# From the router to the experts: a normalised row in halves, a weight piece split earlier, gate products begun on half of their input, and fills left out

## What is computed

```python
h2l = modulate(rms_norm(xl, norm_ffn[l]), sh2, sc2)
xl = xl + g2 * moe_ffn(h2l, w_router, b_router, *experts)
...
def moe_ffn(h, w_router, b_router, w_gate, w_up, w_down):
    aff = jax.nn.sigmoid((tok @ w_router).astype(jnp.float32))
    biased = (aff + b_router.astype(jnp.float32)).reshape(n_tok, N_GROUPS, EXPERTS_PER_GROUP)
    ...
    def expert_block(args):
        xb, e = args
        hb = jax.nn.silu(xb @ w_gate[e]) * (xb @ w_up[e])
        return hb @ w_down[e]
```

## Time and profile before

| | |
|---|---|
| runs | 2020.72, 2022.87, 2019.8 us |
| the profiled execution | 2017.9 us |
| its span | 2016.2 us |
| TensorE (PE) busy | 1964.6 us |
| VectorE (DVE) busy | 1717.3 us |
| ScalarE (ACT) busy | 1162.6 us |
| mean over the span, DMA | 312 GB/s |
| mean granted clock of TensorE | 0.995 |

### The profile page before, as it was taken

How to read it: one execution, slowest core, us unless ns; L and a number is a source line. 1 busy time by engine, 2 the same in 40 slices (tenths; PEclk the granted TensorE clock), 3 DMA queues, 4 the chain that set the end, 5 groups by cost and what they waited for, 6 DMA issues and landing times.

```text
span 2016.2 us, 25838 instructions
## 1 busy us (share of the span) xinstructions
PE 1964.6 (97%) x9392; PEld 1566.4 (78%) x9392; DVE 1717.3 (85%) x1731; ACT 1162.6 (58%) x1134; POOL 196.5 (10%) x254
## 2 busy tenths in 40 slices
PE   7999999999999999999999998999999999999996
PEld 3788558778888888888888577677888888888885
DVE  4775789898689999999999988777799999999997
ACT  2324613323367777777777355344477777777774
POOL 3000110111030000000000300100100000000001
PEclk9999999999999999999999999999999999999998
DMA  9766417666489999999999677286799999999995
GB/s 347 269 238 224 143 67 240 244 221 252 183 284 410 391 406 392 397 392 398 396 400 390 250 254 250 64 328 222 271 391 390 399 395 397 391 403 387 405 388 219
DMA packets 181489, 629.45 MB, mean 312 GB/s; under 512 B 13903, under 2 KB 16091, under 8 KB 174368
## 3 DMA queue, kind: packets, MB, share of 16 engines
q1 hardware_dynamic: 150648, 503.62, 66.1%
q0 software_dynamic: 27808, 119.98, 16.2%
q10 hardware_dynamic: 2952, 4.77, 0.6%
HBM read 597.13 MB, written 31.19 MB: 312 GB/s over the span
## 4 chain that ended last, share of the span: by engine, by line
PE 83%; DVE 9%; DMA 5%; ACT 2%; issue 1%; SPq 1%; POOL 0%; ACTq 0%; DVEq 0%; POOLq 0%
PE bank L2517 78%; PE bank L2527 4%; DVE work L1693 3%; DMA ring<-in_w_mod_dram 1%; DVE m_lo L1693 1%; DVE ring L1693 1%; PE bank L2790 1%; DMA ring<-in_w_in_dram 1%; DMA work<-hp_dram 1%; DMA ring<-in_w_exp_down_dram 1%; DVE work L2073 1%; DVE w_lo L1693 1%; DMA x<-in_ctx_dram 1%; DMA ring<-in_w_out_dram 1%; ACT work L1444 0%
## 5 line engine op out<-in xcount | busy, mean ns | idle before, releaser
L1693 DVE TENSOR_TENSOR w_lo<-ring,w_hi 128x2048 fp32r<-128x2048 f32 x384 | 873.6, 2289 | 87.8 <-ACT w_hi L1556 86.2
L1556 ACT ACTIVATE w_hi<-ring 128x2048 fp32r<-128x2048 f32 x384 | 738.0, 1922 | 237.1 <-PE bank L2517 232.1
L2517 PE MATMUL bank<-w_hi,xsT_hi 128*128 128x512 f32 x1024 | 399.8, 390 | 0.8 <-DVE w_lo L1693 0.6
L2517 PE MATMUL bank<-w_lo,xsT_hi 128*128 128x512 f32 x1024 | 398.6, 389 | 0.0
L2517 PE MATMUL bank<-w_hi,xsT_lo 128*128 128x512 f32 x1024 | 315.4, 389 | 0.0
L1276 ACT ACTIVATE m_hi<-ring 128x1024 fp32r<-128x1024 f32 (+1 forms) x128 | 129.8, 1031 | 262.2 <-PE bank L2517 211.9
L2517 PEld LDWEIGHTS bank<-w_hi,xsT_hi 128*128 128x128 f32 x1024 | 192.2, 188 | 44.9 <-issue 1.9
L2517 PEld LDWEIGHTS bank<-w_hi,xsT_lo 128*128 128x128 f32 x1024 | 192.2, 188 | 40.2
L2517 PEld LDWEIGHTS bank<-w_lo,xsT_hi 128*128 128x128 f32 x1024 | 192.2, 188 | 38.6
L2517 PE MATMUL bank<-w_hi,hexpT_hi 128*128 128x512 f32 x512 | 202.3, 395 | 0.6 <-DVE w_lo L1693 0.6
L2517 PE MATMUL bank<-w_lo,hexpT_hi 128*128 128x512 f32 x512 | 199.5, 390 | 0.0
(11 more groups left out here) (304 smaller groups left out, 2634.5 us busy)
## 6 DMA issues: line engine op xcount, KB each, us to landing
ring<-in_w_exp_gate_dram SPq DMA_DIRECT2D x128, 1024.0 KB, 9.1
ring<-in_w_exp_up_dram SPq DMA_DIRECT2D x128, 1024.0 KB, 7.9
ring<-in_w_exp_down_dram SPq DMA_DIRECT2D x128, 1024.0 KB, 8.6
ring<-in_w_in_dram SPq DMA_DIRECT2D x44, 1024.0 KB, 7.3
work<-in_w_mod_dram POOLq DMA_DIRECT2D x40, 1024.0 KB, 5.6
ys_dram<-work POOLq DMA_DIRECT2D x32, 512.0 KB, 7.8
work<-hp_dram SPq DMA_DIRECT2D x54, 256.0 KB, 4.4
work<-mod_dram POOLq DMA_DIRECT2D x8, 1024.0 KB, 9.5
```

Of the source, the lines that this page charges most:

```text
L1556: nc.scalar.activation(w_hi[:, pos % N_SPLIT, :], raw(i), ACT.Copy).then_inc(hi_done, 1)
L1693: return nc.vector.tensor_tensor(o, a, b, op)
L2517: return nc.tensor.matmul(o, a, b, start=first, stop=last)
```

## The change

Eight edits.

1. `in_halves` is true for layer 0's last block alone. There `modulated_halves` makes the row in two halves of 512 columns, counting a new semaphore `half_row` for the first and `rows_ready` for the second; `turn_row` waits for each in turn.
2. For the same block `high(0, 0)` stands in front of the squares in ScalarE's order, and waits for `split_used` (two quarters of the last output products are done) in place of `dve_took`.
3. `logits` waits for each half of `hT` before its four matmuls, for all blocks and layers.
4. The two fills in front of layer 0's last logits are dropped.
5. `gate_up` of expert 0 waits for the first half of `xt_lo` before piece 0 and for the second before piece 2, in both layers; its three fills are dropped.
6. In layer 1 the two fills between the merged rows' transposes are dropped.
7. In layer 1 the two fills in front of each half of block 0's output products are dropped.
8. The semaphore `zero_rows` goes; its one use counts on `zero_ready`.

```diff
+def in_halves(l, k):
+
+    return l == 0 and k == len(tokens_of(l)) - 1
...
-                    nc.gpsimd.memset(ys[:, 1, :], 0.0).then_inc(zero_rows, 1)
-                    pool.wait_ge(zero_rows, 1)
+                    nc.gpsimd.memset(ys[:, 1, :], 0.0).then_inc(zero_ready, 1)
+                    pool.wait_ge(zero_ready, 3)
...
+                    if isinstance(e, int) and e == 0 and p == 0 and turned_gates(l):
+                        act.wait_ge(split_used, 3 * SPLIT_NO[("o", l, 1)] + 2)
+                    elif isinstance(e, int) and ready_at(e, p) <= N_SPLIT:
...
                 for k, tb in enumerate(T):
+                    if in_halves(l, k):
+                        high(0, 0)
                     act.wait_ge(dve_took, TAKEN[("o", l, 1, tb)])
                     square_of(2 * l + 1, k, tb, h2row[k])
...
-                high(0, 0)
+                if not in_halves(l, len(T) - 1):
+                    high(0, 0)
...
+            def modulated_halves(row, k, tb):
+
+                ends = (half_row, rows_ready)
+                for n in range(2):
+                    cols = slice(n * CH, (n + 1) * CH)
+                    link(nc.vector.scalar_tensor_tensor(out=row[:, cols], in0=x[:, tb, cols], scalar=stat[:, 3, k:k + 1],
+                                                        in1=A_bc[:, tb // 2, cols], op0=ALU.mult, op1=ALU.mult))
+                    TT(row[:, cols], row[:, cols], B_bc[:, tb // 2, cols], ALU.add).then_inc(ends[n], 1)
...
-                    modulated(h2row[k], k, tb)
+                    if in_halves(l, k):
+                        modulated_halves(h2row[k], k, tb)
+                    else:
+                        modulated(h2row[k], k, tb)
...
                         b = begin("hT", l, p, tb, half)
+                        by_half = p == 1 and in_halves(l, k)
                         if half == 0:
                             keep_busy(b, fill_of(p, k))
+                            if by_half:
+                                pe.wait_ge(half_row, 1)
+                        if half == int(by_half):
                             pe.wait_ge(rows_ready, ROWS_AT[l, p] + k + 1)
...
                         if half == 0:
-                            keep_busy(b, 2 * k)
                             pe.wait_ge(merged_ready, 2 * T_BEFORE[l] + nt + k + 1)
...
-                        keep_busy(b, 2 if tb == T[-1] else 4 if l == 0 else 8)
-                    pe.wait_ge(act_took, TAKEN[("hT", l, 1, tb, 1)])
+                        keep_busy(b, (2 if l else 0) if tb == T[-1] else 4 if l == 0 else 8)
                     for k in range(KB):
+                        if k % 4 == 0:
+                            pe.wait_ge(act_took, TAKEN[("hT", l, 1, tb, k // 4)])
...
-                            if l and k == 0:
-                                keep_busy(b, 2)
...
                     if first:
-                        keep_busy(bank[1], 3)
-                        pe.wait_ge(xt_lo, 2 * Lb + 2)
+                        pe.wait_ge(xt_lo, 2 * Lb + 1)
                     for p in range(8):
                         up = p // 4
+                        if first and p == 2:
+                            pe.wait_ge(xt_lo, 2 * Lb + 2)
```

More of the change, by code:

```diff
@@ L651, in hybrid_kernel @@
         final_ready = sem("final_ready")
-        zero_rows = sem("zero_rows")
+        half_row = sem("half_row")
         zero_rows_stored = sem("zero_rows_stored")
@@ L1530, in _ @@
                         next(ahead)
-                for k, tb in enumerate(T):
-                    act.wait_ge(dve_took, TAKEN[("o", l, 1, tb)])
-                    square_of(2 * l + 1, k, tb, h2row[k])
-                    root(2 * l + 1, k, 1, k)
-                    if k >= 2:
-                        logits(l, T[k - 2])
-                    if k:
-                        transposed(l, T[k - 1])
                 loaded = base_loads[l]
@@ L1550, in high @@
                         act.wait_ge(slot_loaded[i], e * 32 + 16 * (loaded[i] + (p - 4 - i) // N_RAW + 1))
-                    if isinstance(e, int) and ready_at(e, p) <= N_SPLIT:
+                    if isinstance(e, int) and e == 0 and p == 0 and turned_gates(l):
+                        act.wait_ge(split_used, 3 * SPLIT_NO[("o", l, 1)] + 2)
+                    elif isinstance(e, int) and ready_at(e, p) <= N_SPLIT:
                         act.wait_ge(dve_took, TAKEN[("o", l, 1, T[-1])])
@@ L1556, in high @@
                     nc.scalar.activation(w_hi[:, pos % N_SPLIT, :], raw(i), ACT.Copy).then_inc(hi_done, 1)
+                for k, tb in enumerate(T):
+                    if in_halves(l, k):
+                        high(0, 0)
+                    act.wait_ge(dve_took, TAKEN[("o", l, 1, tb)])
+                    square_of(2 * l + 1, k, tb, h2row[k])
+                    root(2 * l + 1, k, 1, k)
+                    if k >= 2:
+                        logits(l, T[k - 2])
+                    if k:
+                        transposed(l, T[k - 1])
                 nc.scalar.activation(c_raw[:, 1, l:l + 1], c_raw[:, 1, l:l + 1], ACT.Sigmoid)
-                high(0, 0)
+                if not in_halves(l, len(T) - 1):
+                    high(0, 0)
                 logits(l, T[-2])
```

## The result

The changed kernel takes 2026.85 us (median of 19 executions, 2021.65 to 2033.05), the kernel before 2020.75 (median of 19, 2019.26 to 2024.61). The ratio is **1.0026, with an interval of 1.0019 to 1.0033**: slower by about 6 us, where I had forecast 0.6 less and put 0.06 on slower by over 0.2%. The range (2017.9 to 2023.4) does not hold it. The profiled execution has a span of 2027.4 us, 11.2 more than the one of before.

The account below looks back on a forecast made before the run. TensorE, busy for 97% of the span, was taken as the bound, so only its waits could shrink: +0.4 us in layer 0 and -1.0 in layer 1 gave -0.6 on the 2020.72 median, or 2020.1 us (range 2017.9 to 2023.4).

Parts of the forecast that it names:

- Split moved ahead of the square, +2.35: Layer 0's last row: ScalarE's split waits for the first weight piece, so the square starts 2.35 us later.
- Router +0.95 net: Layer 0's router: late square against the gain from halves, logits taken 0.95 us later in all.
- priced at -1.4: Layer 0's last row made in two halves: alone this saves 1.4 us up to the logits being taken.
- The two fills dropped before the last logits ...: 0 for time.: Layer 0: these fills stood where TensorE waits for hT, so dropping them changes the time by 0.
- First gate products: Expert 0, both layers: products start on the first half of xsT_lo, 1.45 us earlier in layer 0.
- the landing decides at 611: Layer 0: a weight piece's landing at 606.60 ends the stretch, so TensorE's start at 611 shifts by +0.4 us.
- Layer 1's -1.0: Layer 1: earlier gate products shorten the stretch to 1469 us by 1.0 us, with no landing in the way.
- Fills of layer 1, 0: Layer 1: six fills dropped around merged rows and output projection save 0, since a w_out wait follows.
- The second place that rival A gave: Layer 1's merged-row transposes without fills: clock may fall, 0 to 1.7 us, taken as 0.5; 0.05 of that rival's chance.
- rival A: Layer 0: TensorE's clock falls in the thinned stretch, 1.7 us of work undone, 2021.8 or 2023.5 us; chance 0.27.
- its -0.6: Whole kernel: layer 0's +0.4 and layer 1's -1.0 add up to 0.6 us less.

Follow-up runs that it names:

- e2: Changed kernel with five more fills ahead of the third block's logits in layer 0 (9 in place of 4); ratio 1.0006 to the kernel before.
- e7: Kernel before with only layer 0's last row made by halves, the split in its old place; median 2021.54 us, ratio 0.9999.
- e5: Kernel before with only the fills dropped, in layer 0 and layer 1; median 2023.37 us, ratio 1.0007.
- e16: Changed kernel with the two fills in front of layer 0's last logits put back; median 2026.57 us, ratio 1.0021 to the kernel before.
- e6: Kernel before with only the early gate products in both layers, the three fills in front of them dropped; median 2020.54 us, ratio 0.9995.

## Why the prediction was wrong, point by point

- **Split moved ahead of the square, +2.35.** Right in kind, 0.4 short: 2.77. The piece lands 5.17 us after its issue, where I had 4.8 from the bytes; the seven other profiles with the split ahead of the square have 5.20 to 5.44.
- **Router +0.95 net.** The delay net of the halves is +1.75 (e2). The halves were priced at -1.4 with ScalarE free for the copy, which only the moved split gives; in its old place they give 0.22 (e7). With the split in its new place, e2's square is 2.81 late and its sigmoid 1.75, so there they give 1.06.
- **"The two fills dropped before the last logits ...: 0 for time."** Alone they bring no fall and 0.07 us until the sigmoid (e5, 9.40 against 9.33). With a low clock it may not be: with them the falls are 3.41 to 6.83 us in three profiles, without them 6.83 to 13.65 in six. The total shows nothing of it (e16).
- **First gate products.** Start 1.45 earlier: 1.65 (e6). That the landing decides at 611 was right. Layer 1's -1.0 was right: -1.12.
- **Fills of layer 1, 0.** Right for the median as far as it can be read. The second place that rival A gave by the Trainium skill (TensorE: Matmul & The Clock Gate, "Part 4: PE-mode transpose"), the transposes of the merged rows without fills, shows as a fall in four of ten profiles, but three of these come behind a stop among full products, not at the transposes, and the fourth begins in the full products right behind them.
- **The step that failed is the clock: the sum has no term for it, and rival A, which had one, was too small** and given too small a chance. I had named the place, the cause (4 us of nothing but 16-column logits, the square late by over 2 us) and the mark (0.5 between 543 and 551), and put 0.27 on it. But I took the length from the one fall of the trace, 0.43 of 4 us or 1.7 us of work. The real one is 13.65 us, and it takes (14.32 - 11.08) + (7.85 - 5.37) = 5.7 us, 3.4 times as much. I also had not counted that a low clock turns cover into path: the twelve fills in front of the counts are as long as the selection at full clock, so at half clock 2.5 us of them stand in front of it. I had written that they "are slowed" and not priced it by itself.
- **The rest of the sum** came out near its -0.6, in part by luck. e2 starts 2.32 us later after the landing than the kernel before; its own fall of 3.41 us at half clock can be up to 1.7 of this, and layer 1 gives 1.12 back, which leaves about -0.5. This is an estimate, and the landings alone vary by more. The parts did not come out so well: the router was 0.8 worse than priced, and the gain at the first product did not show behind the landing.
- **Chances.** By rival A's own condition ("it decides when the square is late by over 2 us") my forecast of +2.35 already met it, so it should have been the likeliest case.

## What to carry to other kernels

A wait moved to an idle place on one engine is paid by whoever is behind it on another: ask what TensorE does for those microseconds, not only when the row comes. When a stop beside thin matmuls is likely, price a fall of the clock over the work that follows without a gap, cover included, and not by the one fall in the trace: here the falls lasted for 3.41 to 13.65 us. A gain in front of a queue of landings is not a gain until the landing moves; the same edit gave 1.1 us in the layer where no landing followed.

## What had not been expected of the hardware

The granted clock stayed at half for 13.65 us while TensorE was busy for all of the 13.65; being busy with transposes, 16-column logits and a few fills did not bring it back. In three profiles with two fills more among them it was 3.41 or 6.83 us, but one without them had 6.83 too. Two executions of one kernel differed too (13.65 and 10.24 us), and falls of 3.41 or 6.83 us between the layers were in some profiles and not in others of kernels that are alike there. The executions of the kernel before spread by 9 and 11 us (2018.04 to 2026.63 in one series of 35, 2018.91 to 2029.74 in another), so parts of 1 us had to be read from the traces, stretch by stretch, and not from medians.
